# The second FFN product of a streaming layer, by seven block products instead of eight

## The chip, the cores and the metric

One core of one Trainium2 chip runs the whole program. The metric is the device time of one launch in microseconds (us); less is better. TensorE is called PE in the profile, VectorE DVE, ScalarE ACT, GpSimd POOL and SyncE SP. SP computes nothing here and only starts DMAs, in program order.

## What is computed

One transformer layer for 1024 prompt rows and 64 sample rows of 1024 features, in fp32. The change touches how the last lines are computed:

```python
merged = g_a * (y_a @ w_branch_a) + g_b * (y_b @ w_branch_b)
x  = x + rms_norm(merged @ w_o, g_post_mix)
up = rms_norm(x, g_pre_ffn) @ w_up          # 1024 -> 2*2816
conv = causal depthwise convolution (width 3) of up; gate, val = split(conv)
ff = (gelu(gate) * val) @ w_down            # 2816 -> 1024
x  = x + rms_norm(ff, g_post_ffn)
```

## The kernel before

The program is a row of stages, each a block of its own with a barrier of all engines at its end. The last three are the merge stage (`phase_merge`), the output stage (`phase_output`: `merged @ w_o`, both norms, transposition of the result, and the first products with `w_up`) and the FFN stage (`phase_ffn`). Each engine's instructions stand in the order in which they are written; semaphores tie the engines together.

Every product is made in three passes of TensorE: each fp32 operand is split into a high part (rounded by ScalarE or GpSimd, `w_hi`, `hid_hi`) and the remainder (`w_lo`, `hid_lo`, by VectorE or GpSimd), and `three_passes` (L170 to L174) multiplies high by low, high by high and low by high.

The merge stage has 24 chunks of 364 columns in 8 feature tiles of 3 chunks. SP loads the tiles of `w_branch_b` (`Weights.load`, L146), GpSimd splits them (`split_one`, L152 and L155), PE multiplies (L297), VectorE gates and adds, ScalarE and VectorE split the result into `mergedT`. When the weights are in, SP starts the four first loads of `w_o` (L2459). The output stage begins by splitting those.

The FFN stage first makes the 22 feature tiles f of the hidden layer (`product`; each tile's rows are stored in DRAM as `hid_scratch`, L3185). The second product follows, called the down stage below (`down`, with the loads in `load_raw` and `load_hid`). It takes the nine row tiles (eight of 128, one of 64) in teams of 4, 3 and 2 (`TEAMS`), and for each team walks through all 22 f (`PASSES`, 66 in all). A pass loads 128x1024 of `w_down` and the team's hidden columns, ScalarE and VectorE split both, and PE multiplies each row tile by both halves of the output columns. Weights are kept in a ring that is four blocks of 1024 deep (`FFN_SLOTS`), hidden parts in two places. After each team the sums in PSUM are squared, scaled by `g_post_ffn`, normalised and added to the row of x (`square`, `evacuate`, `normalise`, `finish`); for the last team this stands behind the last matmul, half by half (`square_half`, `begin_root`, `evacuate_half`, `root_of`).

Around the seam of the two parts of the FFN stage, ScalarE's list reads: value row of the last tile (`begin_value`), weights of pass 2, gate row (`begin_gate`), weights of pass 3, hidden part of pass 2, and so on. VectorE's list has the evacuations of the last product (`c22`, `c12`), then the two convolutions, then the splits for passes 3 and 4.

## Time and profile before

| | us |
|---|---|
| median of 3 runs (2135.84 to 2137.24) | 2136.28 |
| the profiled execution, its own time | 2138.59 |
| its span, first to last instruction | 2136.8 |
| merge stage, PE at work | about 1156 to 1247.8 |
| FFN stage, hidden layer by `product` | about 1460 to 1849 |
| down stage, first to last matmul | 1848.9 to 2127.75 |
| behind the last matmul | 9.1 |

The span is the time between the first and last recorded instruction; 1.8 us of the execution lie outside it. PE is busy for 97% of the span. Busy times of matmuls overlap (one begins before the one ahead of it ends), so what a matmul costs in a dense stretch is the distance from start to start.

### The profile page before, as it was taken

How to read it: one execution, taken by the hardware profiler on the slowest of the kernel's cores; microseconds unless marked ns; L12 is line 12 of the kernel's file. 1: busy time of each engine (PE TensorE's matmuls, PEld its weight loads, DVE VectorE, ACT ScalarE, POOL GpSimd, SP SyncE). 2: the span in 40 equal slices, each digit the busy share in tenths (PEclk: the TensorE clock that was granted, in tenths of full speed). 3: DMA queues.
4: the chain of work that ended last, by engine and by line, in shares of the span. 5: the costliest groups of instructions: out<-in, count | busy, mean ns of one | idle time of the engine just before them, and what ended most of it. 6: DMA issues, size and time to landing. Idle time of an engine off the chain costs nothing. (4 is left out here: it accounts for less than half of the span.)

```text
span 2136.8 us, 35593 instructions
## 1 busy us (share of the span) xinstructions
PE 2070.1 (97%) x13704; PEld 1953.3 (91%) x13704; DVE 1419.5 (66%) x2242; ACT 958.1 (45%) x1773; POOL 742.8 (35%) x499
## 2 busy tenths in 40 slices
PE   5999999998999999999999999999999999999998
PEld 5998999998899999998999978899999999988875
DVE  5956544443787788857556557598888888834565
ACT  4334534433777777754342122243333333423343
POOL 2333355554644454436565210003333334100000
PEclk9999999999999999999999999999999999999999
DMA  5434344768546555546666433311222222563654
GB/s 175 116 98 133 131 166 166 206 187 238 150 120 144 125 131 142 136 149 176 190 183 205 157 126 99 89 61 61 72 74 79 67 86 62 194 206 127 217 183 163
DMA packets 313278, 298.65 MB, mean 140 GB/s; under 512 B 51767, under 2 KB 275991, under 8 KB 313111
## 3 DMA queue, kind: packets, MB, share of 16 engines
q1 hardware_dynamic: 299776, 265.61, 42.8%
q10 hardware_dynamic: 11094, 22.65, 2.9%
q0 software_dynamic: 2240, 8.13, 1.0%
q8 instruction: 109, 1.79, 0.4%
q14 instruction: 59, 0.48, 0.1%
HBM read 210.03 MB, written 86.30 MB: 139 GB/s over the span
## 5 line engine op out<-in xcount | busy, mean ns | idle before, releaser
L1786 DVE TENSOR_TENSOR_SCAN p_rest<-p_rest 128x896 f32<-128x896 f32 (+7 forms) x128 | 215.0, 1692 | 78.4 <-ACT p_rest L1705 78.4
L1555 POOL TENSOR_TENSOR p_weights<-p_weights,p_rest 128x895 f32<-128x895 f32 (+7 forms) x128 | 162.4, 1275 | 202.6 <-DVE p_rest L1786 202.6
L3355 DVE TENSOR_TENSOR p_w_lo<-p_w_raw,p_w_hi 128x512 fp32r<-128x512 f32 (+1 forms) x168 | 161.0, 963 | 54.4 <-ACT p_w_hi L3147 54.3
L3147 ACT ACTIVATE p_w_hi<-p_w_raw 128x512 fp32r<-128x512 f32 (+1 forms) x186 | 139.3, 772 | 68.0 <-DVE p_rows L3374 37.0
L172 PE MATMUL p_psB<-hT_lo,w_hi 128*128 128x274 f32 (+2 forms) x528 | 161.4, 306 | 4.2 <-issue 2.4
L174 PE MATMUL p_psB<-hT_hi,w_lo 128*128 128x274 f32 (+2 forms) x528 | 159.2, 302 | 0.0
L173 PE MATMUL p_psB<-hT_hi,w_hi 128*128 128x274 f32 (+2 forms) x528 | 159.1, 301 | 0.0
L172 PE MATMUL ps_up<-mergedT_lo,p_w_hi 128*128 128x274 f32 (+1 forms) x488 | 149.2, 306 | 4.1 <-DVE p_rows L3438 1.7
L1130 DVE TENSOR_TENSOR p_x<-p_psB,p_x 128x274 f32<-128x274 f32 (+1 forms) x168 | 70.6, 436 | 118.8 <-PE p_psB L174 113.0
L174 PE MATMUL ps_up<-mergedT_hi,p_w_lo 128*128 128x274 f32 (+1 forms) x488 | 148.4, 304 | 0.0
L173 PE MATMUL ps_up<-mergedT_hi,p_w_hi 128*128 128x274 f32 (+1 forms) x488 | 148.3, 304 | 0.0
L3163 ACT ACTIVATE p_rows<-p_rows,par 128x1090 f32<-128x1090 f32 x44 | 57.2, 1302 | 143.7 <-DVE p_rows L3461 91.6
L3364 DVE SCALAR_TENSOR_TENSOR p_rows<-p_rows,par 128x1090 f32<-128x1090 f32 x88 | 119.2, 1354 | 3.1
L1705 ACT ACTIVATE p_rest<-p_psZ 128x512 f32<-128x512 f32 (+1 forms) x192 | 95.0, 495 | 58.3 <-PE p_psZ L1621 33.2
L1794 DVE TENSOR_TENSOR p_aT<-p_psT,p_aT 128x128 fp32r<-128x128 f32 (+1 forms) x192 | 97.9, 544 | 10.9 <-ACT p_aT L1715 9.8
L172 PEld LDWEIGHTS p_psB<-hT_lo,w_hi 128*128 128x128 f32 x528 | 100.4, 190 | 5.1 <-issue 5.0
L3380 DVE TENSOR_TENSOR p_hid_lo<-p_hid,p_hid_hi 128x512 fp32r<-128x512 f32 (+2 forms) x66 | 35.1, 535 | 104.5 <-ACT p_hid_hi L3195 104.4
L3195 ACT ACTIVATE p_hid_hi<-p_hid 128x512 fp32r<-128x512 f32 (+2 forms) x66 | 33.2, 506 | 155.0 <-PE p_psD L174 131.8
L173 PEld LDWEIGHTS p_psB<-hT_hi,w_hi 128*128 128x128 f32 x528 | 100.9, 191 | 0.2 <-issue 0.2
L174 PEld LDWEIGHTS p_psB<-hT_hi,w_lo 128*128 128x128 f32 x528 | 100.2, 190 | 0.0
L1715 ACT ACTIVATE p_aT<-p_psT 128x128 fp32r<-128x128 f32 (+1 forms) x192 | 85.1, 491 | 29.9 <-PE p_psT L1634 25.7
L172 PEld LDWEIGHTS ps_up<-mergedT_lo,p_w_hi 128*128 128x128 f32 x488 | 91.7, 188 | 6.0 <-issue 2.9
(456 smaller groups left out, 7053.1 us busy)
## 6 DMA issues: line engine op xcount, KB each, us to landing
p_w_raw<-in_w_down SPq DMA_DIRECT2D x66, 512.0 KB, 3.8
p_w_raw<-in_w_up SPq DMA_DIRECT2D x44, 512.0 KB, 5.1
hid_scratch<-p_rows ACTq DMA_DIRECT2D x22, 545.0 KB, 2.9
p_raw_more<-in_w_in SPq DMA_DIRECT2D x20, 512.0 KB, 5.2
w_raw<-in_w_in SPq DMA_DIRECT2D x20, 512.0 KB, 5.3
p_kT<-k_hi_scratch SPq DMA_DIRECT2D x32, 256.0 KB, 4.7
p_kT<-k_lo_scratch SPq DMA_DIRECT2D x32, 256.0 KB, 5.2
w_raw<-in_w_gate SPq DMA_DIRECT2D x16, 512.0 KB, 5.0
```

The lines of the kernel that those rows point to most:

```text
L172: nc.tensor.matmul(out, stat_hi, mov_lo, start=first, stop=False)
L173: nc.tensor.matmul(out, stat_hi, mov_hi, start=False, stop=False)
L174: return nc.tensor.matmul(out, stat_lo, mov_hi, start=False, stop=last)
L1130: nc.vector.tensor_tensor(out, bank(q, STEPS.index(step), i), term, ALU.add).then_inc(s("post"), 1)
L1555: nc.gpsimd.tensor_tensor(wt[:, b % 6, 0:n - 1], wt[:, b % 6, 0:n - 1], rest[:, b % 4, 1:n], ALU.mult).then_inc(s("weights"), 1)
L1705: nc.scalar.activation(rest[:, b % 4, c:c + n], src, ACT.Sigmoid, scale=-SCALE).then_inc(s("nb"), 1)
L1715: nc.scalar.activation(aT[:, k % 2, 0:n, 0, half * P:(half + 1) * P], psT[:, half, 0:n, :], ACT.Copy).then_inc(s("aT_hi"), 1)
L1786: nc.vector.tensor_tensor_scan(src, src, src, 1.0, ALU.mult, ALU.bypass).then_inc(s("scanned"), 1)
L1794: nc.vector.tensor_tensor(aT[:, k % 2, 0:n, 1, q], psT[:, half, 0:n, :], aT[:, k % 2, 0:n, 0, q].bitcast(F32), ALU.subtract).then_inc(s("a ...
L3147: nc.scalar.activation(target(w_hi, key), source(key), ACT.Copy).then_inc(s("w_hi"), 1)
L3355: nc.vector.tensor_tensor(target(w_lo, key), source(key), target(w_hi, key).bitcast(F32), ALU.subtract).then_inc(s("built"), 1)
L3364: ins = nc.vector.scalar_tensor_tensor(out=ck[:, GAP:COLS], in0=xk[:, j:COLS - GAP + j], scalar=par[:, PAR[f"w_conv{j}"] + at:PAR[f"w_conv ...
```

## The change

The down product is now a 2x2 by 2x2 block product of seven instead of eight block multiplications. The rows of the prompt form two halves (row tiles 0 to 3 and 4 to 7), even and odd f form the two halves of the inner dimension, and the output columns form two halves of 512. `DOWN` names the seven products, each of 11 passes (f in pairs), 77 passes in all. A pass takes one 128x512 block of weights or weight sums, one 128x512 block of hidden values or of their sums, and four row tiles: 12 matmuls. The 64 sample rows are no part of this; their four plain block products are made by three more matmuls in the passes of P1, P6, P5 and P4 (for the last two three passes later, `LAG`).

Four kinds of weight sums are needed (`weight_sums`: 4 operations of GpSimd for each pair of f). Nine of the eleven pairs are made in the merge stage: SP loads two 512 KB tiles of `w_down` for a pair, GpSimd works in place, SP stores the two tiles to `down_sums_scratch`; two pairs of buffers alternate. They lie where tiles 6 and 7 of `mergedT` go, so ScalarE and VectorE wait for the stores before they write those. The last two pairs are made in the output stage in four rounds of 256 columns. The sums of hidden blocks are made by GpSimd in the down stage as they stream in (`chained`): one operation in each pass of P7, P6, P5 and P3. P7 and P6 keep them in `chain`, of which SP loads eleven more blocks.

VectorE takes each product out of PSUM after its last pass (`evict`, one or two operations for each row tile, seven banks in turn), and the norm of tiles 4 to 8 is now done during the last product, that of tiles 0 to 3 two tiles at a time behind it. The sample's hidden columns are loaded by themselves and split by `sample_hi` and `sample_lo`; the first of these stands ahead of the convolutions of the last hidden tile.

```diff
+MERGE_SUMS = 9
+def weight_sums(nc, pool, sem, n, even, odd):
+    top, right, low, corner = even[:, 0, :], even[:, 1, :], odd[:, 0, :], odd[:, 1, :]
+    nc.gpsimd.tensor_tensor(top, right, top, ALU.subtract).then_inc(sem, 1)
+    nc.gpsimd.tensor_tensor(right, right, corner, ALU.subtract).then_inc(sem, 1)
+    pool.wait_ge(sem, 4 * n + 2)
+    nc.gpsimd.tensor_tensor(corner, corner, top, ALU.subtract).then_inc(sem, 1)
+    pool.wait_ge(sem, 4 * n + 3)
+    nc.gpsimd.tensor_tensor(low, corner, low, ALU.subtract).then_inc(sem, 1)
...
@@ phase_merge
+    SUMS_AFTER = {2: 1, 3: 1, 4: 2, 5: 2, 6: 2, 7: 1}
...
+                def load_sums(p):
+                    if p >= 2:
+                        sp.wait_ge(s(f"sums_stored{p % 2}"), 32 * (p // 2))
...
+                def store_sums(p):
+                    sp.wait_ge(s("down_sums"), 4 * p + 4)
...
                 for n in range(FIRST, KT):
-                    ring.load(sp, n - FIRST, n % 2, w_b[:, :, n * P:(n + 1) * P], KT)
+                    if n + 2 < KT:
+                        ring.load(sp, n + 2 - FIRST, n % 2, w_b[:, :, (n + 2) * P:(n + 3) * P], KT)
+                    for _ in range(SUMS_AFTER[n]):
+                        store_sums(p)
+                        if p + 2 < MERGE_SUMS:
+                            load_sums(p + 2)
+                        p += 1
...
                     ring.split_one(pool, n - FIRST, (n - FIRST) // 2, n % SLOTS, n % 2)
+                    for _ in range(SUMS_AFTER[n]):
+                        pool.wait_ge(s(f"sums_loaded{p % 2}"), 32 * (p // 2 + 1))
+                        weight_sums(nc, pool, s("down_sums"), p, *quarters(p))
+                        p += 1
+                for b in range(2):
+                    pool.wait_ge(s(f"sums_stored{b}"), 32 * ((MERGE_SUMS + 1 - b) // 2))
...
+                    if n >= KT - 2 and c == 0:
+                        act.wait_ge(s(f"sums_stored{(n + 1) % 2}"), 32 * ((MERGE_SUMS + 1 - (n + 1) % 2) // 2))
@@ phase_ffn
-    TEAMS = ((0, 1, 2, 3), (4, 5, 6), (7, 8))
-    PASSES = [(g, f) for g in range(len(TEAMS)) for f in range(FT)]
+    FP = FT // 2
+    DOWN = ("P1", "P7", "P6", "P5", "P4", "P2", "P3")
+    PASSES = [(j, p) for j in range(len(DOWN)) for p in range(FP)]
+    TEAM = 4
+    SUMMED = ("P7", "P6", "P5", "P3")
+    LAG = {"P1": 0, "P6": 0, "P5": 3, "P4": 3}
+    HID = 8
+    BRAW = 8
...
+                def load_chain(p):
+                    if p >= 2:
+                        sp.wait_ge(s("chained"), p - 1)
+                    sp.dma_start(chain[:, p, :], hid_part(2 * p, 1)).then_inc(s(f"chain_ready{p % 2}"), 16)
...
+                def chained(i):
...
+                    x, y = chain[:, p, :], raw_a(i)
+                    dst, left, right, op = {"P7": (x, x, y, ALU.subtract), "P6": (x, x, y, ALU.add), "P5": (y, y, x, ALU.add),
+                                            "P3": (y, y, x, ALU.subtract)}[name]
+                    nc.gpsimd.tensor_tensor(dst, left, right, op).then_inc(s("chained"), 1)
...
                     ready(key)
                     pe.wait_ge(s("split_lo"), i + 1)
-                    at, base = place(key) // 2, team_cols(g).start
-                    for m in team:
+                    for _, e in (x for x in SAMPLED if x[0] == i):
+                        sample(e)
+                    for t in team:
+                        if p == 0:
+                            free(j, t)
...
+                        last = three_passes(nc, down_bank(j, t), operand_a(a_hi, i)[:, c], operand_a(a_lo, i)[:, c], target(w_hi, key),
+                                            target(w_lo, key), p == 0, p == FP - 1)
...
+                def sample(i):
...
+                    if p == 0:
+                        pe.wait_ge(s("sample_lo"), lows)
...
@@ VectorE, seam
+                split_lo(2)
+                weight_lo(("down", 3))
+                sample_lo(0)
+                split_lo(3)
+                weight_lo(("down", 4))
                 convolve(FT - 1, 1)
...
@@ VectorE, passes
+                for i in range(8, N):
+                    if i % FP == 4 and i > FP:
+                        evict(i // FP - 1)
...
+                    if i == 67:
+                        root_of(slice(TEAM, TILES), 2 * TEAM + 2)
+                    if 68 <= i < 68 + TEAM:
+                        scale_row(TEAM + i - 68)
+                    if 69 <= i < 69 + TEAM:
+                        finish(TEAM + i - 69)
+                    if i == 74:
+                        scale_row(SAMPLE)
+                        finish(SAMPLE)
+                    split_lo(i - 1)
                     weight_lo(("down", i))
...
+                split_lo(N - 1)
+                evict(DOWN.index("P3"))
...
@@ evict, last product
+                        if name == "P3":
+                            scale_right(t)
+                        if name == "P3" and t % 2:
+                            root_of(slice(t - 1, t + 1), 3 * TEAM + 2 + t + 1)
+                            dve.wait_ge(s("x2_upper"), 16 * TEAM)
+                            finish_half(t, 1)
+                            finish_half(t - 1, 1)
+                            finish_half(t, 0)
+                            finish_half(t - 1, 0)
```

VectorE at the seam before: the last evacuations (L3461), the two convolutions (L3360 to L3364), then splits of weights (`p_w_lo`) and hidden columns (`p_hid_lo`).

```order
L3355 TENSOR_TENSOR p_w_lo<-p_w_raw,p_w_hi 128x1024
L3461 TENSOR_TENSOR p_rows<-p_psD,p_snap 128x274
L3461 TENSOR_TENSOR p_rows<-p_psD,p_snap 128x272
L3360 COPY p_tails<-p_rows 128x2
L3361 COPY p_tails<-p_rows 128x2
L3362 COPY p_rows<-par 128x2
L3364 SCALAR_TENSOR_TENSOR p_rows<-p_rows,par 128x1090 x2
```

VectorE at the same place now; `p_a_lo` is the low part of a hidden block, `p_sample_split` that of the sample's columns.

```order
L3585 TENSOR_TENSOR p_w_lo<-p_w_raw,p_w_hi 128x512
L3699 TENSOR_TENSOR p_rows<-p_psD,p_snap 128x274
L3699 TENSOR_TENSOR p_rows<-p_psD,p_snap 128x272
L3608 TENSOR_TENSOR p_a_lo_19414<-p_hid_19409,p_a_hi_19412 128x512
L3585 TENSOR_TENSOR p_w_lo<-p_w_raw,p_w_hi 128x512
L3614 TENSOR_TENSOR p_sample_split_19416<-p_sample,p_sample_split_19416 128x704
```

Five operations now stand between the weights of pass 2 and the end of the sample's split. PE at the same seam now, from the last matmul of the hidden layer on:

```order
L175 MATMUL p_psD<-mergedT_hi,p_w_lo 128x272
L173 MATMUL p_psD<-p_w_lo,p_sample_split_19416 64x512
L174 MATMUL p_psD<-p_w_hi,p_sample_split_19416 64x512
L175 MATMUL p_psD<-p_w_hi,p_sample_split_19416 64x512
L173 MATMUL ps_up<-p_w_lo,p_a_hi_19411 128x512
```

The sample's matmuls stand first in pass 0. SP in the merge stage before: six tiles of `w_branch_b`, then `w_o`.

```order
L2452 UNCONDITIONAL_BRANCH
L146 DMA p_w_raw<-in_w_branch_b 128x8x128 x6
L2459 DMA p_w_raw<-in_w_o 128x2x512 x4
L2450 UNCONDITIONAL_BRANCH
```

SP at the end of the merge stage now (`p_down` are the buffers of the pairs):

```order
L2488 DMA down_sums_scratch<-p_down_16834 128x1024
L2488 DMA down_sums_scratch<-p_down_16835 128x1024
L2483 DMA p_down_16834<-in_w_down 128x1024
L2483 DMA p_down_16835<-in_w_down 128x1024
L2488 DMA down_sums_scratch<-p_down_16836 128x1024
L2488 DMA down_sums_scratch<-p_down_16837 128x1024
L2488 DMA down_sums_scratch<-p_down_16834 128x1024
L2488 DMA down_sums_scratch<-p_down_16835 128x1024
L2506 DMA p_w_raw<-in_w_o 128x2x512 x4
```

The four loads of `w_o` moved behind the stores of all nine pairs.

## Rows read from the trace of the kernel before

**Rows 1.** The page, part 1: busy us (share of the span) xinstructions.

```profile
PE 2070.1 (97%) x13704; PEld 1953.3 (91%) x13704; DVE 1419.5 (66%) x2242; ACT 958.1 (45%) x1773; POOL 742.8 (35%) x499
```

**Rows 2.** Busy by stretch: us, PE, PEld, DVE, ACT, POOL, granted clock, DMA share, GB/s.

```profile
1460.00:1845.00 385.00, 381.36 (x2992) 378.40 (x2991) 315.38 (x529) 148.77 (x221) 143.66 (x105) 1.00 0.25 79
2000.00:2050.00 50.00, 50.00 (x216) 40.30 (x215) 21.04 (x24) 17.29 (x25) 0.00 (x0) 1.00 0.57 182
1156.00:1244.00 88.00, 87.93 (x530) 87.96 (x531) 46.84 (x66) 11.21 (x22) 25.20 (x14) 1.00 0.52 162
1162.00:1168.00 6.00, 6.00 (x38) 6.00 (x37) 4.70 (x6) 1.01 (x2) 5.66 (x4) 1.00 1.08 355
```

**Rows 3.** Down stage, instructions by form: xcount, busy us, mean ns, idle before.

```profile
L3355 DVE TENSOR_TENSOR p_w_lo<-p_w_raw,p_w_hi 128x1024 fp32r<-128x1024 f32 x65 | 79.6, 1225 | 25.2 <-ACT p_w_hi L3147 25.1
L172 PE MATMUL p_psD<-p_w_lo,p_hid_hi 128*128 128x512 f32 x176 | 69.8, 397 | 0.1
...
L172 PE MATMUL ps_up<-p_w_lo,p_hid_hi 128*64 128x512 f32 x44 | 17.3, 394 | 0.0
L3380 DVE TENSOR_TENSOR p_hid_lo<-p_hid,p_hid_hi 128x512 fp32r<-128x512 f32 x22 | 15.1, 689 | 60.9 <-ACT p_hid_hi L3195 60.9
```

**Rows 4.** PE's waits in the down stage: us in total, times, longest.

```profile
PE ps_up L172 <- DVE p_hid_lo L3380: 0.6, 1, 0.6
```

**Rows 5.** PE's timeline, down stage: start us, duration, engine, line, operation, tiles.

```profile
1848.91 0.40 PE L172 MATMUL ps_up<-p_w_lo,p_hid_hi 128*128 128x512 f32 x1
...
1851.71 0.40 PE L172 MATMUL p_psD<-p_w_lo,p_hid_hi 128*128 128x512 f32 x1
```

**Rows 6.** Timeline of ScalarE, then VectorE, at the seam.

```profile
1848.79 1.30 ACT L3163 ACTIVATE p_rows<-p_rows,par 128x1090 f32<-128x1090 f32 x1 [3.74 <-DVE p_rows L3455]
1849.99 1.04 ACT L3147 ACTIVATE p_w_hi<-p_w_raw 128x1024 fp32r<-128x1024 f32 x1
...
1851.07 1.23 DVE L3355 TENSOR_TENSOR p_w_lo<-p_w_raw,p_w_hi 128x1024 fp32r<-128x1024 f32 x1 [1.97 <-ACT p_w_hi L3147]
1852.21 0.78 DVE L3461 TENSOR_TENSOR p_rows<-p_psD,p_snap 128x274 f32<-128x274 f32 x2
```

**Rows 7.** PE's waits of the whole span, and a stretch's clock (as rows 2).

```profile
PE p_psZ L1617 <- DMA p_kT<-k_lo_scratch: 3.4, 1, 3.4
...
519.80:521.50 1.70, 1.70 (x7) 1.70 (x6) 0.00 (x0) 1.09 (x2) 0.00 (x0) 0.50 1.23 284
```

**Rows 8.** Timeline from the last matmul to the last DMA.

```profile
2127.36 0.40 PE L174 MATMUL ps_up<-p_w_hi,p_hid_lo 128*64 128x512 f32 x1
...
2129.73 0.14 DVE L3503 SCALAR_TENSOR_TENSOR p_mean<-p_half_ss,p_mean 64x1 f32<-64x1 f32 x1
...
2131.74 1.41 DVE L3632 SCALAR_TENSOR_TENSOR p_x<-p_acc,p_rstd,p_x 64x512 f32<-64x512 f32 x2
...
2133.24 0.53 ACTq L3344 DMA_DIRECT2D out_y_sample<-p_x  x1
```

**Rows 9.** Merge stage, timelines of GpSimd, VectorE, PE and ScalarE.

```profile
1177.57 2.56 POOL L155 TENSOR_TENSOR w_over<-p_w_raw,w_over 128x1024 fp32r<-128x1024 f32 x1
...
1177.79 2.73 DVE L2516 TENSOR_TENSOR mergedT_lo<-p_ta,mergedT_hi 128x364 fp32r<-128x364 f32 x1
...
1247.44 0.49 PE L297 MATMUL p_ps<-yT_hi,w_over 128*128 128x364 f32 x2
1248.23 0.63 ACT L2679 ACTIVATE p_w_hi<-p_w_raw 128x512 fp32r<-128x512 f32 x1 [2.58 <-PEq L2450]
```

**Rows 10.** Landing time of 512 KB in the merge stage; a stretch with many stores (as rows 2).

```profile
p_w_raw<-in_w_o SPq DMA_DIRECT2D x8, 512.0 KB, 5.8
...
2081.00:2088.00 7.00, 7.00 (x32) 4.75 (x31) 4.07 (x6) 3.23 (x5) 0.53 (x1) 1.00 1.04 410
```

**Rows 11.** Forms of one size: GpSimd, whole span; VectorE, 1460 to 1845 us.

```profile
L3023 POOL TENSOR_TENSOR p_w_raw<-p_w_raw 128x512 f32<-128x512 f32 x18 | 23.4, 1299 | 69.5 <-DVE p_w_lo L3355 69.5
...
L3355 DVE TENSOR_TENSOR p_w_lo<-p_w_raw,p_w_hi 128x512 fp32r<-128x512 f32 x89 | 72.0, 810 | 27.8 <-ACT p_w_hi L3147 27.8
```

More of the change, by code:

```diff
@@ L2800, in phase_ffn @@
     INDEX = {key: n for n, key in enumerate(BUILDS)}
-    SIZE = [2 if key[0] == "down" else 1 for key in BUILDS]
-    PLACE = list(itertools.accumulate([4] + SIZE))
+    PLACE = [4 + n for n in range(len(BUILDS))]
     OWNER = {}
-    for key, at, size in zip(BUILDS, PLACE, SIZE):
-        for x in range(size):
-            OWNER[at + x] = key
+    for key, at in zip(BUILDS, PLACE):
+        OWNER[at] = key
     def by_pool(key):
@@ L2816, in earlier @@
     def earlier(key):
[L2818 to L2819 removed]
+        return OWNER.get(PLACE[INDEX[key]] - OPS)
     def fast(f):
         return f - PLAIN
[L2824 to L2825 removed]
     def raw_block(key):
[L2829 to L2830 removed]
         f, j = key
@@ new lines, in load_x2 @@
+                def load_x2(m):
+                    if TEAM + 2 <= m < SAMPLE:
+                        sp.wait_ge(s("finished"), m - TEAM - 1)
+                    sem = "x2_sample" if m == SAMPLE else "x2_upper" if m < TEAM else f"x2_lower{m % 2}"
+                    sp.dma_start(x2_of(m), d.x2[m * P:m * P + rows(m), :]).then_inc(s(sem), 16)
+                for b in range(4, 2 * FT):
+                    load_raw(b)
+                sp.wait_ge(s("t_lo"), 8)
+                load_sample(0, FT - 2, "sample_most")
```

638 lines of the change are left out of this document (403 added, 235 removed).

## The prediction

> **What bounds the kernel now.** The page comes first: PE is busy for 97% of the span [rows 1]. The table of stretches says where that is strict [rows 2]: in the middle of the down stage PE is busy for 50.00 of 50 us while VectorE works 21.04, ScalarE 17.29 and GpSimd nothing; in the merge stage it is busy for 87.93 of 88 us, GpSimd for 25.20, and the DMA engines have half their time free (share 0.52). The waits of PE in the down stage add up to 0.6 us [rows 4]. So the down stage lasts as long as its matmuls, and fewer matmuls shorten it as long as the others keep pace; the merge stage has no room on PE but much beside it.
>
> **The matmuls.** Before there are 66 passes over nine row tiles in all, with two halves and three matmuls: 22 x 9 x 2 x 3 = 1188. Now there are 77 x 4 x 3 = 924 for the prompt and 44 x 3 = 132 for the sample, 1056. All move 512 columns. The busy mean of one is 397 ns for 128 rows and 394 ns for 64 [rows 3], so a sample matmul costs what a prompt one does; the pitch is what counts: twelve matmuls lie between the two starts shown, 2.80 us, 0.2333 us each [rows 5]. 132 fewer are worth 30.8 us. A pass of 12 lasts 2.8 us, one with sample matmuls 3.5.
>
> **The seam, +5.3 us.** Pass 0 begins with the sample's matmuls, and they wait for `sample_lo(0)`. VectorE reaches it behind the low part of pass 2's weights, two evacuations, a hidden split and the weights of pass 3. ScalarE's value row ends its turn at 1849.99, when the weights of pass 2 begin [rows 6]. They are now 512 wide, about half of 1.04 us, and end near 1850.6. VectorE from there, with the 512-wide split at 0.69 [rows 3] and the pair of evacuations 0.78 [rows 6]: 1851.3, 1852.0, 1852.6, 1853.3, and the sample's 704 columns (0.69 x 704/512, some 0.9) to 1854.2. ScalarE is ahead of it by then. PE used to start at 1848.91 [rows 5]: 5.3 us later. It is bounded by 3 (if ScalarE gets past the value row sooner) and 8 (if the hidden blocks of pass 2, queued on SP behind a wait for the last but one hidden tile's store, land late).
>
> **The clock, +1.7 us.** After an idle of 3.4 us on PE, the profile shows a granted clock of 0.50, the level of 1.2 GHz, in the 1.7 us that follow [rows 7]. The stall at the seam is longer. Half speed for the 1.7 us shown loses 0.85; how much longer it lasts at the seam is open, so I take 1.7 us, between 0.85 and 3.5. The Trainium skill ("TensorE: Matmul & The Clock Gate", part 1) has the throttled state as the default that activity releases, which speaks against a change that opens a gap in a dense stage; by the rule this term stands, without it the sum would be 1.7 us less. Rows 7 side with the rule.
>
> **Keeping pace in the down stage, +2 us.** Per pass VectorE has two splits of 512, 0.69 us alone [rows 3], 0.81 beside a GpSimd that is busy 37% of the time [rows 2, 11], and some 0.1 less each back to back: 1.4 of 2.8 us. It may be about three passes ahead: ring and hidden places hold four to eight blocks, and `split_hi` of pass i needs pass i-4 done. Evicting four tiles is 4 or 8 operations of about 0.62, 2.5 to 5 us, and fits in that lead of 8.4 us less 1.6 for the splits. Seven banks free the fourth tile's bank 2 us before it is wanted. The tight place is the last product: between passes 67 and 74 VectorE has root (14 steps of 0.20, pitch from ten steps in 2.01 us [rows 8]), eight scalings, eight additions, an eviction and the sample's row, 2.8 + 5.4 + 5.2 + 2.5 + 2.5 = 18.4 us over the splits' 11, in eight passes of 22.4. The excess of 7 eats the lead. Laid out pass by pass, PE waits 0.5 us at pass 70 and 1.5 in the four last passes, done tile by tile, since all four splits are needed within the first tile. 2 us; 0 with splits at 1.2 a pass, 4 if GpSimd slows them more.
>
> **GpSimd and the streams, 0.** GpSimd has one operation of 1.3 us [rows 11] in 2.8. In P7 a pass loads 768 KB, 281 GB/s, under the 355 and 410 reached [rows 2, 10]. SP waits there for GpSimd before each chain load, so a step is landing plus sum plus issue, about 4.5 us for nine steps; SP is eight passes (22 us) ahead when it begins, since P1 passes last 3.5 us, and ends some 9 us ahead.
>
> **Behind the last matmul, +4.2 us.** Before: 2127.75 to 2136.8, 9.1 us. Now VectorE does tiles 0 and 1 when tile 1 is done (5.6 us before the end): two operations each, root 2.8, four halves of 0.63; it is busy until 1.4 us behind the last matmul. Then tiles 2 and 3: four operations 2.6, ScalarE's squares beside, root 2.8, four halves 2.5, to about 9.6. From the last DMA's issue to the end it was 3.6 us (2133.24 to 2136.8 [rows 8]). 13.2 or 13.3 against 9.1. Between +2 and +6.
>
> **The merge stage, +7 us.** GpSimd adds 36 operations of 1.3 us, 47 us, to 25.2 busy of 88: it fits. The transfers hardly do. The stage moves 162 GB/s for 88 us, 14.3 MB [rows 2]; nine pairs add 9 x (1.05 in + 1.05 out), 18.9 MB. 33.1 MB at 355 GB/s (the best of the stage) are 93 us, at 410 (the best seen, long rows) 81. In the same buffer load, sums and store must follow each other: with 512 KB landing in 5.8 us here [rows 10] I take 5.5 to 7 us for each 1.05 MB under load and 5.4 for the four operations, 17 to 19.5 us for two pairs. From about 1168, four such rounds end the eighth pair at 1236 to 1246, and the ninth's sums 5.4 later. Only then come the four loads of `w_o`, behind a store: 2.6 MB, some 9 us, to 1251 to 1261. ScalarE wanted the first at 1248.23, right behind PE's last matmul of the stage at 1247.44 [rows 9]. +3 to +12; 7 taken. The last tile's split waits behind the eighth pair, to between 1237 and 1244, where PE wants it at 1235.7 (12 us before the end); this stall runs beside, not on top. If transfers reach 410 GB/s the term is 0, if every round takes 21 us it is 18.
>
> The Trainium skill ("DMA: Bandwidth & Descriptors", specifications) gives two ceilings, about 358 GB/s for a core's HBM and 435 for the fabric, and has the first bind for HBM to SBUF. The row of 355 agrees, that of 410 does not, and the measurement decides: it leaves both ends open. By the first the term is at least 5, by the second it would be near 0.
>
> **The output stage, +0.5 us.** Four rounds of four sums of half the size on GpSimd in a stage whose VectorE has slack; each two-input operation of VectorE can wait out one of GpSimd, as L2516 did: 2.73 us against 2.56 of GpSimd's [rows 9]. 0 to 2.
>
> **Sum.** -30.8 + 5.3 + 1.7 + 2.0 + 4.2 + 7 + 0.5 = -10.1 against the profiled execution's 2138.59 (span 2136.8 and 1.8 around it): 2128.5. That execution was 2.3 us above the median of the runs, 2136.28; on the median it is 2126.2.
>
> **Rivals.**
> *Transfers are free.* The merge term is 0 and the seam 3: 2118. For: 410 GB/s [rows 10]. Against: the chain of load, sums and store in two buffers.
> *The merge stage is bound by its chain.* Rounds of 24 us: the ninth pair ends near 1269, `w_o` lands at 1278, 30 late: 2126.2 - 7 + 30 = 2149, slower than before; at 21 us the loads land at 1266, +18, 2137, no change to speak of. It decides from a round of 22. For: 33 MB in a stage that moved 14. Against: rows of 4 KB, the best kind, and the traffic of gates ends near 1230.
> *The port, the other side.* If each of VectorE's two splits waited out a whole GpSimd operation of 1.3 us, a pass of P7, P6, P5 and P3 would take 1.2 + 2.6 = 3.8 us on VectorE: 1.0 more than PE's for 44 passes, less the lead of 7: +37, 2163. It decides from 2.8 us a pass. For: L2516 above. Against: beside GpSimd's 143.66 us [rows 2] the mean of the same split was 0.81, not 2.
> *The hidden stream starves P7.* SP's step at 6 us instead of 4.5: 9 x 1.5 less 9 of lead, 4.5 us: 2131.
>
> **Chances.** The forecast 0.60, with its own range 2120 to 2133; free transfers 0.10; a merge chain of 20 to 22 us 0.09 and one above 0.05; the port 0.05; starved P7 and what else costs 4 to 10 us 0.11. 0.2% is 4.3 us, about what a measurement of this kernel can tell: faster means under 2132.0. The merge chain above 22 us and the port, 0.10, are slower; the slow merge chain, 0.02 of the forecast and 0.03 of the starved cases are the same, 0.14; the rest is faster, 0.76. The range is 2115 to 2136.
>
> **What would show it.** 1056 matmuls at 0.233; a gap of PE near 5 us before the first sample matmul, ended by VectorE, with a lower granted clock behind; a wait of PE or ScalarE at the end of the merge stage, ended by GpSimd or by the load of `w_o`; small waits for VectorE's splits in P3; 13 us behind the last matmul. A down stage longer than 265 us, or waits spread over P7 to P5, would make it wrong.

## The result and the profile after

The changed kernel takes 2162.56 us (median of 4 runs, 2158.61 to 2166.95), the kernel before 2136.76 beside it. The ratio is 1.0118, 95% interval 1.0093 to 1.0143: slower by 1.2%. The forecast was 2126.2, faster, with a range up to 2136.

The profiled execution took 2158.61 us, its span 2156.5. Between marks that both traces have, it divides like this (us, from the rows below and [rows 5, 8, 9]). This execution is the fastest of the four, 4 us under their median, so the pieces add up to 19.6 us and not to the 25.8 between the medians:

| piece | before | after | difference | forecast |
|---|---|---|---|---|
| start to ScalarE's first split of `w_o` | 1248.23 | 1264.82 | +16.6 | +7 |
| to the first matmul of the down stage | 600.7 | 604.7 | +4.0 | +5.8 (seam, output stage) |
| to the end of its last matmul | 278.9 | 273.8 | -5.1 | -27.1 |
| to the end of the span | 9.0 | 13.2 | +4.1 | +4.2 |

Part of the first row is hidden: ScalarE issues the merge stage's first loads at 1152.42, at 1156.03 before, so the merge stage itself lost 20.2.

The page, part 1, and the marks on ScalarE's and PE's timelines:

```profile
PE 2053.3 (95%) x13572; PEld 1940.1 (90%) x13572; DVE 1476.6 (68%) x2310; ACT 953.6 (44%) x1812; POOL 878.6 (41%) x592
...
1264.82 0.63 ACT L2761 ACTIVATE p_w_hi<-p_w_raw 128x512 fp32r<-128x512 f32 x1 [3.25 <-DMA p_w_raw<-in_w_o]
...
1869.55 0.66 PE L173 MATMUL p_psD<-p_w_lo,p_sample_split 128*64 128x512 f32 x1 [4.18 <-DVE p_sample_split L3614]
...
2142.95 0.40 PE L175 MATMUL p_psD<-p_w_hi,p_a_lo 128*128 128x512 f32 x1
```

132 matmuls fewer than in [rows 1], as forecast, and PE is busy for a smaller share. Where it waits (us in total, times, longest):

```profile
PE p_ps L299 <- POOL w_over L156: 13.5, 2, 7.9
PE ps_up L173 <- DVE p_a_lo L3608: 6.5, 6, 2.3
PE p_psD L173 <- DVE p_rows_lower L3715: 6.1, 1, 6.1
PE p_psD L173 <- DVE p_sample_split L3614: 5.3, 2, 4.2
PE p_psD L173 <- DVE p_a_lo L3608: 4.4, 1, 4.4
```

In [rows 4] the whole down stage had one wait of 0.6. The second and the last row (6.5 and 4.4) are waits for a split of hidden values, the fourth (5.3) is for the sample's split, 4.2 at the seam and 1.1 in P6. The stretches say where they are (columns as in [rows 2]; the first answers to that group's merge stage, the last but one to its middle of the down stage):

```profile
1156.00:1244.00 88.00, 79.39 (x461) 78.80 (x459) 54.59 (x58) 9.16 (x18) 62.53 (x42) 0.94 0.90 305
...
1930.00:1962.00 32.00, 20.35 (x67) 14.74 (x66) 26.19 (x22) 10.57 (x18) 23.05 (x15) 0.79 0.79 273
2000.00:2050.00 50.00, 50.00 (x218) 38.46 (x217) 25.89 (x42) 17.30 (x30) 0.00 (x0) 1.00 0.61 189
2100.00:2143.00 43.00, 36.52 (x141) 27.75 (x139) 39.74 (x57) 13.21 (x28) 17.75 (x10) 0.92 0.46 153
```

Three places are wrong: the merge stage, the turn from P7 to P6, and P3. In each GpSimd is busy, and the granted clock is under 1.00.

The down stage is accounted for almost to the end. Its 1056 matmuls at the pitch of [rows 5] are 246.4 us. Behind its first matmul PE waits 18.1 us: 4.4 and 6.1 around the turn from P7 to P6, 1.1 for the sample, 6.5 in P3. Behind the seam's wait, these two and two waits of 2.3 us in P3, matmuls start every 0.43 us instead of 0.233 for 7 to 13 of them, which loses 9.0 us (1.5, 2.6, 2.0, 1.5 and 1.5, from their start times). The sum is 273.5, against 273.8.

**Merge stage.** The DMA engines are busy for 0.90 of the time (0.52 before) and move 305 GB/s over the whole stage, where the 355 and 410 of [rows 2, 10] were short stretches at a share of 1.08 and 1.04. A store lands 8.5 us after its issue, a load 4.8, and in each of the two pairs of buffers load, sums and store follow each other. The transfers by line (count, KB each, median us to landing), then GpSimd's and SP's timelines at the end of the stage:

```profile
p_down<-in_w_down SPq DMA_DIRECT2D x16, 512.0 KB, 4.8
down_sums_scratch<-p_down SPq DMA_DIRECT2D x16, 512.0 KB, 8.5
```

```profile
1223.40 1.44 POOL L2436 TENSOR_TENSOR p_down<-p_down 128x512 f32<-128x512 f32 x1
1224.81 1.04 POOL L153 TENSOR_SCALAR w_over<-p_w_raw 128x1024 fp32r<-128x1024 f32 x1
1225.93 2.34 POOL L156 TENSOR_TENSOR w_over<-p_w_raw,w_over 128x1024 fp32r<-128x1024 f32 x1
...
1244.17 1.26 POOL L2436 TENSOR_TENSOR p_down<-p_down 128x512 f32<-128x512 f32 x1
1245.40 1.04 POOL L153 TENSOR_SCALAR w_over<-p_w_raw 128x1024 fp32r<-128x1024 f32 x1
```

```profile
1245.46 10.54 SPq L2488 DMA_DIRECT2D down_sums_scratch<-p_down  x4
1256.03 3.15 SPq L2506 DMA_DIRECT2D p_w_raw<-in_w_o  x4
```

In GpSimd's list the split of PE's next weights (L153, L156) stands behind the sums of two pairs, so it waits until they have landed and are summed. PE waits for it twice, 7.9 and 5.6 us. Then the loads of `w_o` go out only at 1256.03.

**P7 to P6.** SP's timeline in P7, VectorE's, and GpSimd's at the turn:

```profile
1899.87 0.32 SPq L3131 DMA_DIRECT2D p_chain<-hid_scratch  x1
1900.24 0.42 SPq L3108 DMA_DIRECT2D p_w_raw<-down_sums_scratch  x1
1900.76 0.38 SPq L3126 DMA_DIRECT2D p_hid<-hid_scratch  x1
1905.60 0.32 SPq L3131 DMA_DIRECT2D p_chain<-hid_scratch  x1
```

```profile
1934.11 0.69 DVE L3585 TENSOR_TENSOR p_w_lo<-p_w_raw,p_w_hi 128x512 fp32r<-128x512 f32 x1 [2.70 <-ACT p_w_hi L3364]
1937.19 1.59 DVE L3608 TENSOR_TENSOR p_a_lo<-p_chain,p_a_hi 128x512 fp32r<-128x512 f32 x1 [2.39 <-ACT p_a_hi L3413]
...
1942.70 1.77 DVE L3608 TENSOR_TENSOR p_a_lo<-p_chain,p_a_hi 128x512 fp32r<-128x512 f32 x1
1944.40 1.79 DVE L3585 TENSOR_TENSOR p_w_lo<-p_w_raw,p_w_hi 128x512 fp32r<-128x512 f32 x1
```

```profile
1935.24 1.26 POOL L3208 TENSOR_TENSOR p_chain<-p_chain,p_hid 128x512 f32<-128x512 f32 x1 [5.22 <-DMA p_hid<-hid_scratch]
...
1938.77 19.08 POOL L3208 TENSOR_TENSOR p_chain<-p_chain,p_hid 128x512 f32<-128x512 f32 x11 [0.53 <-DMA p_hid<-hid_scratch]
```

SP's step is 5.7 us here, and 47.9 us for the eight steps between the chain loads at 1882.11 and 1930.05: 6.0 each, against PE's 2.8. The queue's order makes it so. SP issues the hidden block of pass p (L3126) and then the chain load of pass p+2 (L3131), whose gate is the sum of pass p, which needs the hidden block just issued. The next hidden block stands behind that gate. So the chain blocks are two ahead, but only one hidden block is ever on its way, and a step is its landing (3.5 us: issued at 1900.76, its sum begins at 1904.25), the sum (1.3) and three issues (0.9).

PE catches up and waits 4.4 us. When SP is past the chain loads, P6's hidden blocks come one behind the other and GpSimd does eleven sums in 19.08 us without a pause, 1.73 each. The splits of VectorE that begin beside them take about 1.77 instead of 0.69, and PE waits 6.1 us more. This second wait ends with an evacuation and not with a split:

```profile
1956.63 1.87 DVE L3715 TENSOR_TENSOR p_rows_lower<-p_rows_upper,p_psD 128x512 f32<-128x512 f32 x3
...
1957.36 0.80 PE L173 MATMUL p_psD<-p_w_lo,p_a_hi 128*128 128x512 f32 x1 [6.06 <-DVE p_rows_lower L3715]
```

P6's fourth row tile goes into the bank of P7's first one, with seven banks in turn. In VectorE's list that evacuation stands behind P7's last split and those for P6's first three passes, ten operations from 1939.31 on, which is right for an engine that is three passes ahead of PE. They take 17.3 us instead of about 6.4 (eight at 0.60 from start to start, two of the sample at 0.8).

**P3.** VectorE has its own work here besides the splits, and GpSimd has more than the sums of hidden blocks: it also multiplies the left halves of the upper rows by `g_post_ffn`, four operations in a row.

```profile
2119.73 6.77 POOL L3235 TENSOR_TENSOR p_rows_upper<-p_rows_upper,p_g_row 128x512 f32<-128x512 f32 x4
```

Beside these, too, the splits take 1.76 us.

Below, "the port" is short for what the prediction's rival of that name describes, the slowing of VectorE by a GpSimd operation beside it. The rows show the slowing; they don't show what in the chip causes it.

### The profile page after: what moved, and what is told of

Read it like the earlier page. It is cut to its first block and busy times, and to the rows that moved or that the text cites. A ratio compares the mean times of both kernels' runs of the same rounds, so it can differ in the third digit from the quotient of the medians.

```text
span 2156.5 us, 35820 instructions
## 1 busy us (share of the span) xinstructions
PE 2053.3 (95%) x13572; PEld 1940.1 (90%) x13572; DVE 1476.6 (68%) x2310; ACT 953.6 (44%) x1812; POOL 878.6 (41%) x592
## 3 DMA queue, kind: packets, MB, share of 16 engines
q8 instruction: 108, 1.77, 0.3%
## 5 line engine op out<-in xcount | busy, mean ns | idle before, releaser
L3585 DVE TENSOR_TENSOR p_w_lo<-p_w_raw,p_w_hi 128x512 fp32r<-128x512 f32 x179 | 145.8, 819 | 39.3 <-ACT p_w_hi L3364 39.3
L3364 ACT ACTIVATE p_w_hi<-p_w_raw 128x512 fp32r<-128x512 f32 x197 | 117.7, 620 | 74.6 <-DVE p_rows L3604 30.1
L3222 POOL TENSOR_TENSOR p_w_raw<-p_s,p_w_raw 128x512 f32<-128x512 f32 x18 | 23.2, 1291 | 197.7 <-DVE p_w_lo L3585 197.7
L1708 ACT ACTIVATE p_weights<-p_psZ 128x512 f32<-128x512 f32 (+1 forms) x192 | 95.0, 495 | 0.0
```

The source lines that it names most:

```text
L1708: nc.scalar.activation(wt[:, b % 6, c:c + n], src, ACT.Sigmoid, scale=SCALE).then_inc(s("beta"), 1)
L3364: nc.scalar.activation(target(w_hi, key), source(key), ACT.Copy).then_inc(s("w_hi"), 1)
L3585: nc.vector.tensor_tensor(target(w_lo, key), source(key), target(w_hi, key).bitcast(F32), ALU.subtract).then_inc(s("built"), 1)
```

## The experiments

The four runs that take one thing away or shift it come first. Times are medians of 4 to 10 runs; differences without another name are to the changed kernel's 2162.56. The runs stand in three groups (e1 to e4; e5, e6, e7, c1; e8, e9, e11, c2). The kernel before, run beside each group, was at 2135.9, 2137.3 and 2136.3, and at 2136.8 beside the changed kernel, so 1 to 2 us between groups mean nothing. "Down stage" is from its first matmul to the end of its last; the changed kernel has 273.8, and 1056 matmuls at the pitch of [rows 5] are 246.4.

**e1, the merge stage's sums left out.**

```diff
-    SUMS_AFTER = {2: 1, 3: 1, 4: 2, 5: 2, 6: 2, 7: 1}
+    SUMS_AFTER = {n: 0 for n in range(2, KT)}
...
-                    if DOWN[j] in TS_AT:
+                    if DOWN[j] in TS_AT and p < MERGE_SUMS:
+                        src = w_down[...]
+                    elif DOWN[j] in TS_AT:
```

> Left out: the weight sums of the first nine pairs; the merge stage neither loads, sums nor stores them, and the down stage reads blocks of w_down in their place, as many bytes in rows as long. Theory A (the sums' transfers are what the merge stage lost): the first split of w_o starts near 1245 instead of 1264.8, the waits of PE for GpSimd's splits (7.9 and 5.6 us) and the half clock behind them go, the DMA share between 1180 and 1228 falls from 0.91 to about 0.5, and the time falls by about 20 us, to 2141. Rival (the loss is one of order: the loads of w_o and the last split just stand behind other work, and the stage is a few us longer anyway, or the profiled run was unlucky there): less than 8 us. The down stage stays as it is in both.

Measured 2140.0, -22.6. The first split of `w_o` is at 1245.71, GpSimd's waits are gone, and the stage is that of [rows 2] again:

```profile
1152.00:1240.00 88.00, 87.53 (x528) 87.26 (x527) 48.13 (x66) 11.53 (x23) 25.32 (x14) 1.00 0.51 162
```

The down stage keeps its 273.7 us. The sums of the merge stage cost 22.6 us, and the two losses are separate. The run takes away transfers, GpSimd's work and the place in the queues at once; which of them it was is for e5 and e9.

**e2, sums of the down stage cut to 16 columns.**

```diff
-                    nc.gpsimd.tensor_tensor(dst, left, right, op)...
+                    nc.gpsimd.tensor_tensor(dst[:, 0:16], left[:, 0:16], right[:, 0:16], op)...
```

> Left out: of each activation sum on GpSimd in the down stage, all but 16 of 512 columns; waits, signals and transfers stay. Theory B (GpSimd's sums, back to back in P6 and P3, slow VectorE through the operands they share): VectorE's split takes 0.7 us throughout, PE's 6.1 us wait at the start of P6 and its waits in P3 (5 us) go with their half clock: -10 to -14 us, to about 2149. Rival C (the hidden stream starves P7 and what follows is its echo): GpSimd's part of SP's step falls by 1.2 us of 4.5, nine times, 11 us of lead won, so that P7's 4.4 us wait goes too; but VectorE's ops in P6 would then have been slow for another reason and stay at 1.75 us or more. VectorE's durations between 1938 and 1960 tell the two apart: 0.7 for B, 1.75 for C.

Measured 2136.2, -26.4, twice what was expected. The down stage takes 248.0 us, and PE's only waits in it besides the seam's are 1.2 us. Splits from 1930 to 1962 there, by form (xcount, busy, mean ns, idle before):

```profile
L3608 DVE TENSOR_TENSOR p_a_lo<-p_chain,p_a_hi 128x512 fp32r<-128x512 f32 x11 | 7.6, 694 | 14.8 <-ACT p_a_hi L3413 14.8
```

In the changed kernel the same form had a mean of 1731 from 1938 to 1958. The loss of the down stage is the length of GpSimd's sums, nearly all of it. But this run takes some 1.2 us out of SP's step as well, so it doesn't say how much is the port and how much the chain of loads.

**e3, sums held to the pace of the passes.**

```diff
-                    if name == "P6":
-                        pool.wait_ge(s("split_lo"), FP + p + 1)
+                    pool.wait_ge(s("split_lo"), i - 3)
```

> Each activation sum of pass i on GpSimd waits until the split of pass i-4 is done; nothing left out. Theory B (what costs is sums back to back): with one sum of 1.3 us per pass of 2.8 us the split's mean falls from 1.8 to 0.9 or less in P6, the 6.1 us wait of PE at the start of P6 goes, and P3's 5 us shrink to 1 or 2: -6 to -11 us, to about 2153. Rival (a sum costs VectorE the same whenever it runs, or P7's starvation is what counts): less than 3 us. P7's own wait of 4.4 us stays in both.

Measured 2160.95, -1.6: the rival's figure, and no proof of it. The sums are spread where they were to be, and the chain splits' mean falls to 1161 ns from 1940 to 1980. But P7 is starved as before (down stage 277 us), and PE now waits for splits eight times, 18.3 us in all, where it was 10.9. The wait for P7's evacuation did shrink, from 6.1 to 1.8 us, so the spread sums do help there; the gain is lost again elsewhere, likely because GpSimd, held to PE's pace, can't give the other engines a new lead. That reason isn't shown, and the total says nothing on the port's share.

**e4, chain loads further ahead.** Load p waits for the sum of pass p-4 instead of p-2: two passes more, though the expectation calls it three. Three hidden blocks can now be on their way instead of one.

```diff
-                    if p >= 2:
-                        sp.wait_ge(s("chained"), p - 1)
+                    if p >= 4:
+                        sp.wait_ge(s("chained"), p - 3)
...
-                        pool.wait_ge(s(f"chain_ready{p % 2}"), 16 * (p // 2 + 1))
+                        pool.wait_ge(s(f"chain_ready{p % 4}"), 16 * (p // 4 + 1))
```

> The loads of P7's first operands may be three further ahead: load p waits for the sum of pass p-4 instead of p-2. Nothing left out. Theory C (SP waits for each sum before the next load, and this starves P7): PE's 4.4 us wait near 1939 goes, and with it about 2 us of half clock; GpSimd's sums of P6 start while VectorE has a lead, so the 6.1 us wait at 1957 halves: -6 to -9 us, 2154. Rival B (the port alone): P7's wait goes or moves, but P6's sums are bunched as before and PE's wait comes at once behind: less than 3 us.

Measured 2146.0, -16.6: about twice what theory C gave. Down stage 257.6 us (1874.40 to 2131.97). The stretch that was 20.35 busy of 32 is full, although GpSimd works as much in P7 and P6:

```profile
1880.00:1930.00 50.00, 50.00 (x219) 39.22 (x218) 34.46 (x42) 19.21 (x33) 22.21 (x16) 1.00 0.75 254
1930.00:1960.00 30.00, 30.00 (x132) 23.57 (x131) 22.31 (x27) 13.02 (x22) 15.02 (x11) 1.00 0.76 242
```

So the second wait of 6.1 us was not the port's by itself. The port makes VectorE slow; only where the lead over PE was already used up, and the sums came in a heap, did that reach PE. The one gate carries both. What stays is P3: 8.3 us of waits for splits.

**e5, seven pairs in the merge stage.**

```diff
-MERGE_SUMS = 9
+MERGE_SUMS = 7
-    SUMS_AFTER = {2: 1, 3: 1, 4: 2, 5: 2, 6: 2, 7: 1}
+    SUMS_AFTER = {2: 1, 3: 1, 4: 2, 5: 1, 6: 1, 7: 1}
```

with eight rounds in the output stage instead of four, the last two behind its loop.

> Seven pairs of weight sums in the merge stage instead of nine, one behind each tile's split and two behind the fifth tile's, and eight rounds of half pairs in the output stage instead of four; nothing left out. Theory A (the merge stage loses by the amount of transfers and by what stands behind them): 4.2 MB fewer move there, 14 us at 300 GB/s; the last split of GpSimd no longer stands behind two pairs, and the first split of w_o starts near 1250 instead of 1264.8: -12 to -16 us, to 2147. Rival (the rest of the traffic moved there costs the output stage as much, since its VectorE shares with GpSimd): -5 or less, seen as waits in the output stage.

Measured 2147.0, -15.6, as theory A had it: first split of `w_o` at 1249.51, no wait for GpSimd, 91.35 busy of 94 us where it was 80.47. The DMA share is 0.91 still. The transfers fill the stage also with seven pairs, and PE doesn't wait: the share of 0.91 by itself costs PE nothing here. What PE had lost came from what stood in line behind the eighth and ninth pair.

**e6, SP freed from VectorE in P3** (on top of e4; the rows of x for tiles 6 and 7 go into free places of `chain`).

```diff
+                        sp.wait_ge(s("chained"), sum_of(N - FP + 2 * (m - TEAM - 2) + 1))
...
-                    if i in (70, 72):
-                        load_x2(TEAM + 2 + (i - 70) // 2)
+                    if i in (75, 76):
+                        load_x2(TEAM + 2 + i - 75)
```

> On top of e4 (chain loads three further ahead): the residual rows of row tiles 6 and 7 are loaded behind the last activation block, into places of the chain that are free by then, so that SP no longer waits for VectorE at passes 70 and 72; nothing left out. Theory D (P3's activation blocks arrive late because SP waits there, GpSimd's sums bunch up beside the splits that PE is waiting for): GpSimd's P3 sums run from 2070 on, the 8.3 us of PE's waits for splits in P3 shrink to 2 or less: -6 us or more against e4, to 2139. Rival (VectorE's scalings and additions of P3 are too many whatever SP does): -2 us or less.

Measured 2144.0, -2.0 against e4, or -3.4 if each is taken against the kernel before beside it; the intervals of the two overlap, but the down stage, too, is 1.9 us shorter, 255.7. Most sums of P3 come earlier and singly, yet PE waits 3.6 us for an evacuation and 3.1 for splits. Near the rival's figure: theory D fails as the main cause.

**e11, e6 with P3's sums cut to 16 columns.**

```diff
+                    w = slice(0, 16 if name == "P3" else 512)
+                    nc.gpsimd.tensor_tensor(dst[:, w], left[:, w], right[:, w], op)...
```

> e6 with P3's activation sums cut to 16 of 512 columns (left out: the rest of those eleven sums); waits, signals and transfers stay. Theory B: VectorE's long operations between 2060 and 2100 lose 1 us each wherever a P3 sum ran beside, some 10 us, and the 6.7 us of PE's waits in P3 shrink to 1 or 2: -5 to -7 us against e6, 2138. Rival (VectorE's own work in P3, 29 us in eight passes, is too much by itself, as in the working of the prediction): -2 us or less.

Measured 2137.7, -6.3 against e6; down stage 250.4, the waits for splits 2.9. VectorE by form from 2060 to 2110, first in e6, then here:

```profile
L3778 DVE SCALAR_TENSOR_TENSOR p_rows_lower<-p_rows_lower,p_rstd,p_g_row 128x512 f32<-128x512 f32 x8 | 8.7, 1134 | 0.0
```

```profile
L3779 DVE SCALAR_TENSOR_TENSOR p_rows_lower<-p_rows_lower,p_rstd,p_g_row 128x512 f32<-128x512 f32 x8 | 6.7, 874 | 0.0
```

In P3, where VectorE has 29 us of work in eight passes of 2.8, the port is the cause. A shorter sum also lands its block earlier, but in e6 VectorE has no pause from 2080 to 2109, so there it waits for no block. (The 874 still hold GpSimd's four operations on the left halves. PE's remaining waits, 2.9 us, fall beside them and behind.)

**e8, the port by itself.** The kernel before, with idle sums beside its dense down stage.

```diff
+                for n in range(44):
+                    pool.wait_ge(s("passed"), 5 if n < 22 else 8 + n)
+                    nc.gpsimd.tensor_tensor(s1[:], s1[:], s1[:], ALU.subtract).then_inc(s("idle_sums"), 1)
+                    pool.wait_ge(s("idle_sums"), n + 1)
```

> The kernel before, with 44 extra GpSimd operations of 128x512 in the down stage: 22 back to back from the fifth pass on, then one for each of 22 later passes; no transfers are added and nothing is left out. Theory B (a VectorE operation with both operands in SBUF waits out GpSimd's operation that runs beside it): the split of 128x512 goes from 0.7 to about 1.75 us beside the 22 and is mixed beside the spaced ones; VectorE has slack (21 of 50 us busy before), so PE doesn't wait and the time stays within 2 us of 2137. Rival (the long VectorE operations of the changed kernel are the DMA traffic's, or its own buffers'): splits stay at 0.7 here.

GpSimd's 22, and VectorE by form from 1869 to 1905, all with no transfer added:

```profile
1873.81 30.81 POOL L3030 TENSOR_TENSOR p_s<-p_s 128x512 f32<-128x512 f32 x22 [47.52 <-PE p_psD L174]
```

```profile
L3359 DVE TENSOR_TENSOR p_w_lo<-p_w_raw,p_w_hi 128x1024 fp32r<-128x1024 f32 x7 | 13.4, 1913 | 0.3 <-ACT p_w_hi L3151 0.3
L3384 DVE TENSOR_TENSOR p_hid_lo<-p_hid,p_hid_hi 128x512 fp32r<-128x512 f32 x7 | 7.1, 1016 | 19.8 <-ACT p_hid_hi L3199 19.8
```

Against 1225 and 689 in [rows 3], each takes 0.3 to 0.7 us longer, less than one GpSimd operation of 1.04 us (what one takes here when spaced). Theory B's mechanism shows without any transfer; its size of 1.75 does not. Why it is smaller isn't shown: this VectorE idles between splits, and the 22 follow each other every 1.40 us, against 1.73 in the changed kernel. PE stays full beside them (50.00 busy of 50 us from 1880 on). The forecast of the time was off: 2142.7, ratio 1.0029 (1.0017 to 1.0040), 6.4 us more, with 4.1 us of PE's waits for splits instead of 0.6. Of the two new ones, 1.9 us falls among the 22 spaced operations (at 2072) and 1.5 us some 20 us behind them (at 2112); what caused the second, and the other 3 us of the median, isn't resolved.

**e7, the sample's matmuls before the last row tile.**

```diff
-                    for _, e in (x for x in SAMPLED if x[0] == i):
-                        sample(e)
                     for t in team:
+                        if t == TEAM - 1:
+                            for _, e in (x for x in SAMPLED if x[0] == i):
+                                sample(e)
```

> In each pass with sample matmuls PE does them before the last row tile instead of before the first; nothing left out. Theory E (PE's 4.2 us wait at the seam is for the sample's split alone; the prompt operands of pass 0 are ready): nine matmuls, 2.1 us, fill part of the gap: -2 us and up to -1 more from the clock, to 2159. Rival (the prompt operands or banks come no sooner, or the gain is given back in P7, where SP's lead counts and PE has become earlier): 0.

Measured 2161.3, -1.2, within what the two medians are uncertain. At the seam it does its work: the wait falls from 4.18 to 1.9 us. But from the last matmul of the hidden layer to the last of the down stage it is 278.9 us instead of 277.9, in spite of 2.3 us less of this wait: PE is earlier, SP isn't, and the waits around the turn grow (6.5 us for P7's splits, 7.2 for its evacuation, from 4.4 and 6.1). The gain is given back, as the rival had it.

**c1, the four edits together** (e5, e4, e6, e7).

> The four edits together: seven pairs in the merge stage, chain loads three further ahead, the residual rows' loads at the end, the sample's matmuls before the last row tile; nothing left out. If the losses are separate: 2162.6 - 14 - 16.6 - 6 - 2 = 2124, faster than the kernel before (2136). If P7's starvation had been an echo of the merge stage, or one stall hides another: 2132 or more.

Measured 2129.0, ratio 0.9960 (0.9945 to 0.9975). Down stage 257.7 us, from the first prompt matmul and with 1.9 us of the seam's wait inside. The four as measured alone would give 2162.6 - 15.6 - 16.6 - 2.0 - 1.2 = 2127.2: the losses are nearly separate. ScalarE has its first `w_o` only at 1253.53, and PE waits 6.8 us there.

**e9, `w_o` ahead of the last store** (on top of c1).

```diff
+                    if n == KT - 1:
+                        load_w_o()
                     for _ in range(SUMS_AFTER[n]):
                         store_sums(p)
```

> c1 with the four loads of w_o issued before the last store of the merge stage instead of behind it; nothing left out. Theory A (behind the last matmul of the merge stage only their landing is waited for): issue at 1233 instead of 1243.8, the first split of w_o near 1248 instead of 1253.5, PE's wait of 6.8 us shrinks to 3 or less: -4 to -6 us, 2124. Rival (the stage's transfers are the bound, so that what isn't waited for at the loads is waited for at the stores): -1 or less.

Measured 2125.0, ratio 0.9944 (0.9927 to 0.9960); -4.0 against c1. The two intervals overlap, but all four runs lie under all four of c1. SP's and ScalarE's timelines: the loads go out while GpSimd still sums the last pair, whose store follows:

```profile
1228.21 5.31 SPq L2494 DMA_DIRECT2D p_w_raw<-in_w_o  x4
1240.56 0.81 SPq L2488 DMA_DIRECT2D down_sums_scratch<-p_down  x2
```

```profile
1248.32 0.63 ACT L2769 ACTIVATE p_w_hi<-p_w_raw 128x512 fp32r<-128x512 f32 x1 [0.92 <-PEq L2475]
```

ScalarE waits for PE again and not for a load. The order of SP's queue at the end of the stage was worth 5 us of start time (1253.53 to 1248.32).

**c2, e9 with the lower rows' work two passes earlier.**

```diff
-                    if i == 67:
+                    if i == 65:
                         root_of(slice(TEAM, TILES), 2 * TEAM + 2)
```

and so for the squares, scalings and additions.

> e9 with the root, scalings and additions of the lower row tiles two passes earlier; nothing left out. Theory F (VectorE's excess before the last product, lengthened by GpSimd's operations, is the rest of P3's waits, 6.5 us in c1): two passes more, 5.6 us, take in most of it: -3 to -5 us against e9, 2120. Rival (the excess is only moved into P2's passes): 0 against e9.

Measured 2124.6, ratio 0.9945 (0.9931 to 0.9960): the same as e9. The rival is right; VectorE's excess is moved, not taken in: PE's waits for splits in P3 are gone, and the one for an evacuation at the turn to P3 grows from 3.6 to 8.2 us. e9 and c2 beat both kernels: 11 to 12 us under the kernel before, with all seven products and nothing left out.

## Why the prediction was wrong

The matmuls, the seam and the tail came as forecast. Three terms failed. "GpSimd and the streams, 0" took a step of 4.5 us for SP in P7 and nothing behind it; the step was 6.0, and it cost 16.6 us. "The merge stage, +7" took 17 to 19.5 us a round and let GpSimd's late split run beside PE's work; a round took 22.1, PE waited for that split, and it cost 22.6. "Keeping pace, +2" took 0.81 us for a split of VectorE in P3; it was 1.76 beside GpSimd, and the term came to 8.3, 6.3 of it GpSimd's sums.

Point by point, by its own steps:

- **The matmuls, -30.8**: right. 132 fewer, and with the sums cut (e2) the down stage took 248.0 us where 246.4 is the bare pitch.
- **The seam, +5.3, and the clock, +1.7**: right in kind, a little large: 4.18 us of wait, ended by the sample's split. That the clock falls behind the gap shows in the first matmuls, 0.66 us at 1869.55 instead of 0.40; the eight at this level lose 1.5 us. "TensorE: Matmul & The Clock Gate", part 1, in the Trainium skill, calls the throttled state the default. The trace agrees, for it followed most of the new waits, too (granted clock 0.50 from 1939 to 1944), and not the one of 1.1 us. That is why 16.6 us went with e4 and only 11.6 us of waits (4.4, 6.1 and the sample's 1.1): the slow matmuls behind the first two add 4.5, 16.1 in all. The prediction had this term for the seam alone; in the whole down stage it is 9.0.
- **Keeping pace, +2**: wrong in size. P3's waits alone are 6.5 us, 9.5 with the slow matmuls behind them. The step took "0.81 beside a GpSimd that is busy 37% of the time" for all of VectorE's splits, a mean over 385 us, and used it for a stretch in which GpSimd runs back to back and VectorE has no pause. e11 measured the port of P3's sums at 6.3 us by the medians, 5.3 by the down stage.
- **GpSimd and the streams, 0**: the worst miss, 16.6 us (e4). "About 4.5 us for nine steps" was 6.0: 3.5 us of landing, 1.3 of the sum and 0.9 of issues, and in the later steps a sum of up to 1.84, stretched beside VectorE. The rival "the hidden stream starves P7" had just this step of 6, and its 4.5 us is PE's first wait of 4.4. It stopped there. It did not ask what happens when SP comes free: the blocks arrive in a heap, GpSimd sums them back to back, VectorE's splits take 1.77, and PE, with no lead left, waits again. With that, "seven banks free the fourth tile's bank 2 us before it is wanted" fails as well: there was no lead, the evacuation stood behind ten slow operations, and the bank came 6.1 us too late.
- **The port**: the rival's mechanism (a split waits out a GpSimd operation) is true in the rows, with 1.77 where sum and split meet without pause. Its price, 37 us, and its condition, all 44 passes, are not: in e4 GpSimd is busy for 22 of 50 us beside a PE that never waits, because VectorE has time in P7 and P6. Its time of 2163 is that of the result by accident.
- **The tail, +4.2**: right, 13.2 us behind the last matmul against 9.0.
- **The merge stage, +7**: wrong in size and in one step. By e1 it is 22.6. By GpSimd's rows below the four rounds of two pairs took 20.5, 27.0, 23.6 and 17.4 us, 22.1 in the mean, and not 17 to 19.5; the ninth sums begin at 1249.77 where they were to end by 1251. Stores landed in 8.5 us where 5.5 to 7 had been taken for each 1.05 MB; loads, at 4.8, did not take more. That is the rival "the merge stage is bound by its chain" at the point from which it decides. And "this stall runs beside, not on top" failed: PE's two waits for GpSimd's splits, 13.5 us, lie ahead of the last matmul, and the late loads of `w_o` come on top of them, a second queue behind the same stores.

```profile
1161.29 1.30 POOL L2431 TENSOR_TENSOR p_down<-p_down 128x512 f32<-128x512 f32 x1
...
1181.79 1.28 POOL L2431 TENSOR_TENSOR p_down<-p_down 128x512 f32<-128x512 f32 x1 [0.46 <-DMA p_down<-in_w_down]
...
1208.76 1.28 POOL L2431 TENSOR_TENSOR p_down<-p_down 128x512 f32<-128x512 f32 x1 [3.41 <-DMA p_down<-in_w_down]
...
1232.38 1.27 POOL L2431 TENSOR_TENSOR p_down<-p_down 128x512 f32<-128x512 f32 x1 [4.11 <-DMA p_down<-in_w_down]
...
1249.77 1.27 POOL L2431 TENSOR_TENSOR p_down<-p_down 128x512 f32<-128x512 f32 x1 [0.91 <-DMA p_down<-in_w_down]
```

- **The output stage, +0.5**: right; from the first split of `w_o` to the down stage it is 4.0 us more, which the seam's wait accounts for.

The sum with the measured terms: 2136.3 - 30.8 + 4.2 for the seam + 4.1 for the tail + 22.6 merge stage (e1) + 16.6 at P7 and P6 (e4) + 8.3 in P3 (2.0 by e6, 6.3 by e11) = 2161.3, against 2162.6. Differences of medians enter here, with 1 to 2 us of doubt each, so the close agreement is partly luck; the down stage by itself is settled better by its own waits and clock, 273.5 of 273.8. The three that were mis-sized hold 47.5, of which 9 were forecast. The chances treated the rivals as if one excluded the other; a slow merge chain, a starved P7 and the port in P3 came together. (A slip of the working, without effect: free transfers and a seam of 3 give 2116.9, not 2118.)

Open is how the 16.6 of e4 divide between the lead and the port: e3 was to tell and did not. An estimate from the rows: without the slowing, VectorE's ten operations would have ended near 1946, before PE wanted the bank at 1951.1, and the second wait with its slow matmuls, 8.0 us, would not have been; the first, 7.0, would. No run shows this division.

## What to carry to other kernels

When a load is gated by a compute step whose input it is, lay out the step (landing plus sum plus issue) against the consumer's pass, see what else stands behind the gate in the same queue, and follow it past the point at which the gate opens: work that comes in a heap costs again on every engine that it meets. Take an engine's rate beside another from the stretch in which both are dense, not from a mean. Work put into a stage "beside" PE goes behind what PE needs next in each queue it uses (GpSimd's split, SP's loads): count it against that order first, and against busy shares afterwards.
